# Joining the residual with the early half of the output projection: in the attention stage, at the PSUM copy, or in the last stage, on GpSimd

## What is computed

```
h = rms_norm(x, norm1_g)
proj = h @ w_in                       # split into pool, RG-LRU, forgetting attention, stick-breaking attention
y_cat = stack([y_pool, y_lru, y_fox, y_sb])      # four groups of 512 channels
y_cat = rms_norm(y_cat, out_g)        # per group
x = x + y_cat @ w_out                 # w_out is 2048 x 2048
hid = relu(rms_norm(x, norm2_g) @ w_up)
x = x + (hid * hid) @ w_down
```

## Time and profile before

| | |
|---|---|
| median of three runs | 2629.09 us (2624.93 to 2630.58) |
| profiled execution | 2629.09 us |
| its span, first to last instruction | 2627.4 us |
| PE busy | 2535.4 us, 96% |
| DVE, ACT, POOL busy | 1341.3, 914.2, 233.8 us |
| mean granted PE clock | 0.988 of full |
| DMA | 356.75 MB, mean 136 GB/s |

### The profile page before, as it was taken

How to read it: one execution, slowest core, us unless ns; L and a number is a source line. 1 busy time by engine, 2 the same in 40 slices (tenths; PEclk the granted TensorE clock), 3 DMA queues, 4 the chain that set the end, 5 groups by cost and what they waited for, 6 DMA issues and landing times.

```text
span 2627.4 us, 43517 instructions
## 1 busy us (share of the span) xinstructions
PE 2535.4 (96%) x16842; PEld 2331.3 (89%) x16842; DVE 1341.3 (51%) x1860; ACT 914.2 (35%) x1577; POOL 233.8 (9%) x336
## 2 busy tenths in 40 slices
PE   7999999999999969999999999999999999999998
PEld 7999998755555559999999999999999999999998
DVE  6345455335343477454554554554554554554555
ACT  5244455423232334332332332332332332332333
POOL 2060000133333340000000000000000000000000
PEclk9999999999999979999999999999999999999999
DMA  6292222799999852222222222222222222222222
GB/s 204 87 74 94 96 98 82 249 320 361 346 358 348 311 216 83 97 81 97 81 81 97 81 87 91 81 84 94 81 83 95 81 83 95 81 86 91 87 90 101
DMA packets 112866, 356.75 MB, mean 136 GB/s; under 512 B 30489, under 2 KB 34586, under 8 KB 88482
## 3 DMA queue, kind: packets, MB, share of 16 engines
q1 hardware_dynamic: 91906, 286.33, 33.1%
q0 software_dynamic: 20768, 67.65, 7.3%
HBM read 340.20 MB, written 13.74 MB: 135 GB/s over the span
## 4 chain that ended last, share of the span: by engine, by line
PE 85%; DVE 7%; ACT 3%; issue 3%; DMA 2%; SPq 1%; ACTq 0%; DVEq 0%
PE bank L421 47%; PE bank L426 23%; PE bank L1803 4%; PE bank L1745 2%; PE bank L1782 2%; ACT w_hi L408 1%; DMA w_raw<-weights 1%; DVE sum_tmp L490 1%; PE bank L1689 1%; PE bank L1684 1%; DVE w_lo L412 1%; PE bank L1718 1%; PE bank L1692 1%; PE bank L1605 1%; PE bank L1790 1%
## 5 line engine op out<-in xcount | busy, mean ns | idle before, releaser
L421 PE MATMUL bank<-x_act,w_hi 128*128 128x364 f32 (+1 forms) x4848 | 1062.4, 329 | 24.4 <-DVE x_act L502 13.0
L421 PEld LDWEIGHTS bank<-x_act,w_hi 128*128 128x128 f32 x4848 | 774.5, 189 | 27.3 <-issue 14.7
L421 PE MATMUL bank<-hid,w_hi 128*128 128x364 f32 (+1 forms) x3456 | 729.1, 329 | 18.3 <-DVE sum_tmp L490 17.2
L426 PE MATMUL bank<-x_act,w_lo 128*128 128x272 f32 x3232 | 651.0, 288 | 0.0
L490 DVE TENSOR_TENSOR sum_tmp<-sum_tmp,bank 128x544 f32<-128x544 f32 x336 | 241.8, 720 | 721.1 <-ACT sum_tmp L484 721.1
L421 PEld LDWEIGHTS bank<-hid,w_hi 128*128 128x128 f32 x3456 | 555.2, 188 | 28.5 <-DVE sum_tmp L490 25.9
L426 PEld LDWEIGHTS bank<-x_act,w_lo 128*128 128x128 f32 x3232 | 563.8, 189 | 1.3
L483 ACT ACTIVATE sum_tmp<-bank 128x184 f32<-128x184 f32 x336 | 108.6, 323 | 1018.3 <-PE bank L421 1018.2
L426 PE MATMUL bank<-hid,w_lo 128*128 128x272 f32 x2304 | 429.4, 287 | 1.0 <-DVE hid L495 1.0
L412 DVE TENSOR_TENSOR w_lo<-w_raw,w_hi 128x2048 fp32r<-128x2048 f32 x173 | 399.2, 2308 | 44.3 <-ACT w_hi L408 44.3
L426 PEld LDWEIGHTS bank<-hid,w_lo 128*128 128x128 f32 x2304 | 378.9, 188 | 1.8 <-DVE hid L495 1.6
(11 more groups left out here) (226 smaller groups left out, 1596.7 us busy)
## 6 DMA issues: line engine op xcount, KB each, us to landing
w_raw<-weights SPq DMA_DIRECT2D x173, 1024.0 KB, 4.8
k_ring<-fox_k SPq DMA_DIRECT2D x128, 256.0 KB, 5.1
v_ring<-fox_v POOLq DMA_DIRECT2D x128, 256.0 KB, 4.7
k_ring<-sb_k SPq DMA_DIRECT2D x128, 256.0 KB, 5.0
v_ring<-sb_v POOLq DMA_DIRECT2D x128, 256.0 KB, 5.2
wo<-w_early SPq DMA_DIRECT2D x16, 512.0 KB, 6.2
x_in<-xT SPq DMA_DIRECT2D x4, 1088.0 KB, 10.9
kv_out<-proj SPq DMA_DIRECT2D x4, 1088.0 KB, 9.8
```

The costliest lines, as they stand in the source:

```text
L421: ins = nc.tensor.matmul(bank[:, base + b, 0:n], hi, row[:, t:t + n], start=begin, stop=end)
L426: ins = nc.tensor.matmul(bank[:, base + b, 0:HALF], lo, row[:, t:t + HALF], start=False, stop=False)
```

## The change

DVE no longer copies the early product out of PSUM; it adds it to a half tile of `xT` that SP has loaded into the same `xh` slot. So `part` holds the residual plus the early half of the projection. The slot's order becomes load, add, store; the load of half i waits for the store of half i-6. The sum now stands at one place in the DVE program for all units, the later of the two. In stage 3 only `part` is loaded, straight into `x_res`; `x_part`, POOL's 16 additions and the four joins' semaphores are gone, and DVE waits once for all four loads, ahead of its loop over the 16 tiles.

```diff
+        def load_residual(i):
+            if i >= X_SLOTS:
+                sp.wait_ge(xh_stored[i % X_SLOTS], 16 * (i // X_SLOTS))
+            sp.dma_start(xh[i % X_SLOTS][:], half(xT, i)).then_inc(xh_loaded[i % X_SLOTS], 16)
+
         def store_part(i):
-            sp.wait_ge(xh_copied, i + 1)
+            sp.wait_ge(xh_summed, i + 1)
             sp.dma_start(half(part, i), xh[i % X_SLOTS][:]).then_inc(xh_stored[i % X_SLOTS], 16)
 
         for t in range(2):
             load_early_weights(t)
+        for i in range(2):
+            load_residual(i)
         for u in range(2 * DEC_BATCH):
             if u + 1 < 2 * DEC_BATCH:
                 load_keys(u + 1)
...
                 store_part(2 * u - 1)
                 if u + 1 < KT:
                     load_early_weights(u + 1)
+            if u + 1 < KT:
+                load_residual(2 * u + 2)
+                load_residual(2 * u + 3)
...
         for q in (0, 1, 3, 2):
             if q == 2:
                 sp.wait_ge(y_low, 2 * GT)
-            sp.dma_start(x_res[:, 4 * q:4 * q + 4], xT[:, 4 * q:4 * q + 4]).then_inc(xr_in[q], 16)
-            sp.dma_start(x_part[:, 4 * q:4 * q + 4, 0:TOK], part[:, 4 * q:4 * q + 4]).then_inc(part_in[q], 16)
+            sp.dma_start(x_res[:, 4 * q:4 * q + 4], part[:, 4 * q:4 * q + 4]).then_inc(xr_in, 16)
...
-        for t in range(KT):
-            if t % 4 == 0:
-                pool.wait_ge(xr_in[t // 4], 16)
-                pool.wait_ge(part_in[t // 4], 16)
-            nc.gpsimd.tensor_tensor(x_res[:, t], x_res[:, t], x_part[:, t, 0:TOK], ALU.add).then_inc(x_joined, 1)
...
-        def early_copy(i):
-            if i >= X_SLOTS:
-                dve.wait_ge(xh_stored[i % X_SLOTS], 16 * (i // X_SLOTS))
+        def early_sum(i):
+            x = xh[i % X_SLOTS][:]
             dve.wait_ge(wo_done, i + 1)
-            v.tensor_copy(xh[i % X_SLOTS][:], bank[:, 7, 0:HALF]).then_inc(xh_copied, 1)
+            dve.wait_ge(xh_loaded[i % X_SLOTS], 16 * (i // X_SLOTS + 1))
+            v.tensor_tensor(x, x, bank[:, 7, 0:HALF], ALU.add).then_inc(xh_summed, 1)
...
-            between = i < UNITS and not odd and u % 2 == 1
-            if between:
+            if not odd and u < 16 and u % 2 == 1:
                 seq_sums(u)
-                early_copy(i)
...
-            if i < UNITS and not between:
-                early_copy(i)
+            if i < UNITS:
+                early_sum(i)
...
+        dve.wait_ge(xr_in, 64)
         for t in range(KT):
             n = T_OUT + t
             if t % 2 == 0:
                 low_part(dve, C_OUT + t // 2 + 1)
             sum_tile(dve, halves(sum_tmp[n % 2][:]), n)
-            dve.wait_ge(x_joined, t + 1)
             add_to_x(t, n)
...
                 if i >= 1:
-                    pe.wait_ge(xh_copied, i)
+                    pe.wait_ge(xh_summed, i)
```

More of the change, by code:

```diff
@@ L138, in build_step @@
     x_act = at("x_act", [P, KT, 2 * TOK], F32R, A_ACT)
-    x_part = at("x_part", [P, KT, 2 * TOK], F32, A_ACT)
     x_in = at("x_in", [P, KT, TOK], F32, A_PROJ + 5 * SLOT)
@@ L342, in build_step @@
     wo_done = sem("wo_done")
-    xh_copied = sem("xh_copied")
+    xh_loaded = [sem(f"xh_loaded{i}") for i in range(X_SLOTS)]
+    xh_summed = sem("xh_summed")
     xh_stored = [sem(f"xh_stored{i}") for i in range(X_SLOTS)]
@@ L365, in build_step @@
     d_y = sem("d_y")
-    xr_in = [sem(f"xr_in{q}") for q in range(4)]
-    part_in = [sem(f"part_in{q}") for q in range(4)]
-    x_joined = sem("x_joined")
+    xr_in = sem("xr_in")
     sq_in = sem("sq_in")
```

## The result

The kernel after the change takes 2675.19 us (median of four runs, 2669.37 to 2678.57), the one before 2629.84 in the same runs (2624.93 to 2633.92). The ratio is 1.0171, with a 95% interval of 1.0143 to 1.0199: slower by 45 us. The forecast was 2651.9 and its range ended at 2663. The sign was right, the size was not: half of the loss was missing from the sum.

A forecast was written before the change was run, and what follows sets the result against it. PE was taken to set the pace in the attention stage, with DMA just in time. The terms 20.6 + 6.4 + 1 - 5.6 + 0.4 = +22.8 on 2629.1 gave 2651.9 us; range 2641 to 2663.

The forecast's parts named there:

- The moved sum: Attention stage: in eight units the sum comes 2.57 us later, PE gaps become 2.91 us, nothing gives it back; +20.6 us.
- The clock behind the new gaps: Attention stage: PE's clock falls to 1.2 GHz behind some of the eight gaps; half of 0 to 12.7 taken, +6.4 us.
- The price of a fall: Attention stage: one clock fall costs 1.59 us, from 32 L1745 taking 5.31 us behind a 2.99 gap, 3.72 at full clock.
- The bound of 12.7: Attention stage: upper bound of the clock loss, all eight gaps followed by a fall, 8 x 1.59 us.
- R2: Rival, attention stage: the clock falls behind each of the eight gaps, 16.4 + 12.7, so 2658.2 us; chance 0.12.
- The operation: Attention stage: the add from PSUM costs nothing extra over the copy's 0.43 us; at most 1 us over eight places.
- the loads: Attention stage: 32 loads of `xT` halves, 136 KB each, landing in 4 to 5 us, should never hold VectorE.
- the keys: Attention stage: next keys are not issued later; new loads go behind the round's last key, slowing it only at its end.
- the +1 us for DMA: Attention stage: cost taken for the added `xT` load traffic, between nothing and 6.4 us, near the lower end.
- Part 3: Last stage: without POOL's join, tile 0 of the output projection ends earlier; -5.6 us, bounds 3.96 and 6.6.
- The wait for `x_res`: Last stage: the new wait for all four loads, ahead of `low_part` and `sum_tile` of t = 0, costs +0.4 us.
- The upper bound of 3: Last stage: the wait for the four `x_res` loads costs 0 to 3 us if the load lands late.

The follow-up runs named there:

- the first experiment: The changed kernel with the sum of even units of odd rounds put back right behind `seq_sums`, all else as changed; 2621.6 us, ratio 0.9977.
- the join alone: The kernel before without POOL's 16 additions, everything else kept; timed twice: 2624.63 us, ratio 0.9992, then 2619.75 us, ratio 0.9967.

## Why the prediction was right and wrong

**The moved sum: right.** Eight gaps of 2.91 us were forecast from the work put ahead of the sum, eight of 2.91 to 2.92 came, and PE's wait for `xh` grew by 20.6. With the clock kept up the first channel sums are 19.9 later: nothing gives the delay back, as the pair of rounds almost without idle PE time said.

**"The clock behind the new gaps": this step failed**, in both its factors. The price of a fall, 1.59, was read behind the 2.99 gap, where 32 key products of 128 rows follow and the clock was low for 3.4 us of their 5.31. The new gaps have four L1801 and then the scores behind them, products of 8 and 64 rows, and there the low clock lasted 6.8 or 10.2 us: 3.4 or 5.1 us each. I took the length of one low stretch for a constant of the chip. It depends on the work that follows, as the version with dense products first shows (3.4 us of low clock behind the same gap, seven of seven), but not on that alone: behind the gaps of 2.38 us, with the scores next, it was 3.4 twice and 6.8 six times. The count was wrong too: half of the gaps were taken to hold, by the 2.72 row; none did, nor did those of 2.38 us. In place of 4 x 1.59 = 6.4 stands 30.7. With that term mended the sum gives 2629.1 + 20.6 + 30.7 - 5.6 + 0.2 = 2675.0, against 2675.19 measured. That it fits so closely is in part luck: it leaves out 1.6 us more of waits for DMA and the one fall less in the MLP, which about cancel, and the executions spread over 9 us. The bound of 12.7 was no bound, since its price came from a single place with another neighbourhood; so the range, which rested on it, could not hold.

R2, the clock falling behind each gap, was the right mechanism at 0.12, with the same wrong price. The Trainium skill ("TensorE: Matmul & The Clock Gate", section "HAM oscillation — how this bites in real kernels") describes a kernel in which a recurring wait pays the transition every time. The waits there are of some 3 to 5 us, so it doesn't state the same of ours; the trace shows it for 2.91 us, eight of eight. The row that I had set against it, the 2.72 gap that held, was one draw. Every kernel here has that gap, unchanged, at the start of attention; in the eleven traces the clock stays full behind it in five, the kernels before and after among them, and falls in six. PE's timeline there in the first experiment, where the L1661 of the earlier trace rows take 6.25 us in place of 4.92:

```profile
493.77 6.25 PE L1661 MATMUL bank<-const,proj 128*128 128x128 f32 x40 [2.72 <-SPq L390]
```

So that row was no evidence that a gap of this size is safe. And the trace of before held a third row, which I had not read: 6.4 us behind the gap that held comes one of 1.51, for a constant, with short products behind it, and the clock falls there for 3.4 us.

```profile
500.23 0.35 PE L1733 MATMUL bank<-dconst,const 128*96 128x32 f32 x2 [1.51 <-DMA dconst<-dconsts]
```

```profile
502.50:505.00 2.50, 2.50 (x16) 1.11 (x12) 0.00 (x0) 0.00 (x0) 1.08 (x2) 0.50 1.00 364
```

Of the five traces in which the 2.72 gap held, four have a fall behind this shorter one. So two of three places in the trace of before spoke for R2. Why the same gap goes either way, no run here tells.

**The operation, the loads, the keys: right or harmless.** The sum takes 0.43 like the copy. No load of `xh` was waited for; they landed in 4.4 to 8.9 us, median 5.9. PE waited for keys once, 3.4 us against 3.0. Of the +1 us for DMA the trace has two waits for early weights, 1.2 together; with the sum early they were 2.8, with two falls of the clock behind them. Whether the new loads cause them isn't shown: without these loads PE waited 1.1 us for early weights in the old data path with the new place, and 0.4 and 1.8 in the two traces of the join alone.

**Part 3: right.** The join was worth 5.64 us from the first channel sums to tile 0, forecast 5.6, of which 3.89 at PE's first product, forecast 3.96. That the second decimal nearly fits is luck, since other traces give 5.2 to 6.5. The wait for `x_res` cost PE 0.23, forecast 0.4, while VectorE stood idle 4.9 us for it, forecast 5. The upper bound of 3 was real: in the profile of the version with filled gaps a late load left VectorE idle for 7.07 us and PE for 3.24.

```profile
983.84 2.29 DVE L410 TENSOR_TENSOR w_lo<-w_raw,w_hi 128x2048 fp32r<-128x2048 f32 x1 [7.07 <-DMA x_res<-part]
```

## What to carry to other kernels

Where an engine's queue is handed work in the order of its program, moving one 0.4 us instruction behind 2.6 us of others costs the full 2.6 wherever another engine stands right behind it; look at who waits for it, not at its own duration. A gap on a PE that is otherwise full is priced as the gap plus what the low clock behind it costs, and the second part may be the larger (3.8 against 2.57 us here): read it at a gap with the same work before and behind, or take the length of the low stretch as unknown, and never take one gap that held in one trace for a gap that holds. Useless products in the gap are a cheap experiment that parts the two, and here, with the place of the sum undone, the rest of the change is a gain.

## What the runs showed of the hardware

PE gaps of 2.38 us (eight) and of 2.91 to 2.96 us (23, in three kernels) that recur in a full PE brought the granted clock from 2.4 to 1.2 GHz every time in these runs. A gap of 2.72 us that comes once per execution did so in 6 of 11 traces, gaps of 1.76 us in 3 places of 7. No run gives a length that is safe. The eight gaps of 0.46 us behind useless products of 256 columns never did; but a gap of 0.45 us behind products of only 4 columns (L1790) was followed by 3.4 us of low clock, in the first trace of the join alone:

```profile
899.87 1.05 PE L1790 MATMUL bank<-dstat,o_own 128*128 128x4 f32 x8
901.37 1.18 PE L1803 MATMUL bank<-proj,wo 128*128 128x272 f32 x4 [0.45 <-DMA wo<-w_early]
```

So what PE did ahead of the gap seems to count beside its length; no run parts the two. The low stretch lasted 3.4 us behind twelve dense products, and mostly 6.8, at times 3.4 or 10.2, behind scores of 8 and 64 rows. VectorE's operations beside POOL's additions took about 1.5 to 3 times as long (3.41 against 2.29 us, 5.22 against 2.38, and a copy of 128x544 1.46 against 0.44).
